# The last eight expert rows in groups of one, and half an addition on GpSimd, in a hybrid-layer and expert kernel

## The reference, cut to what matters

```python
h = _modulate(x, norm_ffn_g, sh2, sc2)          # 256 tokens x 1024
# per token and per head (8 heads): the 16 best of 128 x 128 experts, by sums of two key scores
# idx: 8 x 16 expert numbers a token; gate: softmax over the 16 scores
act = gelu(h . U[idx]) * gate                   # one dot product of 1024 for each chosen expert
x   = x + g2 * sum(act * V[idx])                # weighted sum of the chosen experts' value rows
```

## Time and profile before

| what | value |
|---|---|
| median of 3 runs | 1267.8 us (1267.05 to 1268.56) |
| the profiled execution, its own time | 1268.92 us |
| its span, first to last instruction | 1267.0 us |
| PE busy | 1140.1 us, 90% |
| DVE busy | 865.2 us, 68% |
| ACT busy | 311.8 us, 25% |
| POOL busy | 331.8 us, 26% |
| mean granted TensorE clock | 0.990 |
| the expert rows in the span | from about 603 us to the end |

### The profile page before, as it was taken

One profiled execution on the slowest core, in us unless ns is written; L12 is line 12 of the kernel. 1 busy time (PEld: TensorE's weight loads), 2 busy tenths in 40 slices (PEclk: granted clock), 3 DMA queues, 4 the chain that ended last, 5 costly groups with the idle time before them and its releaser, 6 DMA issues.

```text
span 1267.0 us, 14106 instructions
## 1 busy us (share of the span) xinstructions
PE 1140.1 (90%) x4824; PEld 696.8 (55%) x4824; DVE 865.2 (68%) x2320; ACT 311.8 (25%) x1005; POOL 331.8 (26%) x285
## 2 busy tenths in 40 slices
PE   9999999989999999999999899999777777777777
PEld 6866658767856678786656454554232323323322
DVE  2758735566445787863897777777778777777665
ACT  0125300244111232421232222232222222222222
POOL 0000000000011000000444544545644544454430
PEclk9999999999999999999999999999999999999999
DMA  8851256833145566454999999999999999999995
GB/s 337 312 202 67 100 199 253 309 112 133 67 199 196 208 216 227 191 194 173 373 377 423 423 424 423 423 423 424 424 423 424 423 423 424 423 423 423 423 424 215
DMA packets 54022, 389.10 MB, mean 307 GB/s; under 512 B 8088, under 2 KB 9624, under 8 KB 14784
## 3 DMA queue, kind: packets, MB, share of 16 engines
q0 software_dynamic: 37792, 269.63, 51.4%
q1 hardware_dynamic: 16160, 118.59, 24.6%
HBM read 387.12 MB, written 1.07 MB: 306 GB/s over the span
## 4 chain that ended last, share of the span: by engine, by line
PE 52%; DMA 34%; DVE 10%; ACT 2%; issue 1%; POOL 0%; SPq 0%; DVEq 0%; ACTq 0%
PE bank L566 15%; PE bank L560 13%; DMA wring<-peer_uv_in,arena 11%; DMA arena<-peer_uv_in,arena 9%; PE bank L1153 9%; DMA const<-peer_uv_in,arena 8%; DMA hT<-peer_uv_in,arena 5%; PE bank L1048 2%; PE bank L595 2%; PE bank L968 2%; DVE arena L1644 1%; PE bank L641 1%; DVE arena L1652 1%; PE bank L627 1%; PE bank L791 1%
## 5 line engine op out<-in xcount | busy, mean ns | idle before, releaser
L1153 PE MATMUL bank<-arena 128*128 128x512 f32 x424 | 202.6, 609 | 40.9 <-ACT arena L1609 40.8
L1153 PE MATMUL bank<-wring,arena 128*128 128x512 f32 x376 | 179.1, 610 | 38.8 <-ACT arena L1609 38.8
L566 PE MATMUL bank<-hT,wring 128*128 128x256 f32 (+1 forms) x896 | 172.5, 351 | 1.0 <-ACT arena L1393 1.0
L2442 POOL TENSOR_TENSOR small<-small,const 128x1 f32<-128x1 f32 (+3 forms) x18 | 16.7, 927 | 566.8 <-DVEq L1656 260.1
L2371 DVE CUSTOM_DVE_ANT_0 arena<-arena 128x1024 f32<-128x1024 f32 x106 | 129.3, 1223 | 50.8 <-DMA arena<-peer_uv_in,arena 50.6
L566 PEld LDWEIGHTS bank<-hT,wring 128*128 128x128 f32 x896 | 150.2, 190 | 24.3 <-issue 8.4
L1153 PEld LDWEIGHTS bank<-arena 128*128 128x128 f32 x424 | 78.2, 194 | 150.4 <-issue 80.8
L2481 POOL DMA_INDIRECT arena<-peer_uv_in,arena x104 | 124.8, 1200 | 132.9 <-PE bank L1153 110.8
L2371 DVE CUSTOM_DVE_ANT_0 wring<-wring,arena 128x1024 f32<-128x1024 f32 x94 | 114.7, 1221 | 44.0 <-DMA wring<-peer_uv_in,arena 43.8
L2481 POOL DMA_INDIRECT wring<-peer_uv_in,arena x94 | 113.9, 1211 | 110.1 <-PE bank L1153 98.8
L1153 PEld LDWEIGHTS bank<-wring,arena 128*128 128x128 f32 x376 | 68.3, 191 | 134.7 <-issue 69.9
(11 more groups left out here) (250 smaller groups left out, 1526.7 us busy)
## 6 DMA issues: line engine op xcount, KB each, us to landing
wring<-w_in SPq DMA_DIRECT2D x22, 2048.0 KB, 8.2
wring<-ada_in SPq DMA_DIRECT2D x12, 2048.0 KB, 9.2
wring<-wo_in SPq DMA_DIRECT2D x5, 2048.0 KB, 7.9
wring<-br_in SPq DMA_DIRECT2D x2, 2048.0 KB, 9.3
arena<-pq_in SPq DMA_DIRECT2D x2, 2048.0 KB, 9.8
wring<-w1b_in SPq DMA_DIRECT2D x2, 1120.0 KB, 8.8
const<-const_in SPq DMA_DIRECT2D x1, 2188.5 KB, 17.8
arena<-cmp_in SPq DMA_DIRECT2D x2, 1024.0 KB, 10.9
```

Source lines behind the costliest of these rows:

```text
L566: ins = pe.matmul(bank[:, at:at + n_tok], w[:, k, col:col + P], rhs[:, k, :], start=(k == 0), stop=(k == KC - 1))
L1153: ins = pe.matmul(sums_of[half][:, :], diag[:, at % NDIAG, :], v_row[slot_of[at]][:, half * 512:(half + 1) * 512], start=(n == 0), stop=(n ...
```

## The change

The first hunk gives the product of tile 1, half 0, a tile of its own, `last_scaled`. The second makes rows 248 to 255 eight groups of one (before only 254 and 255 were). The third and fourth take the addition of tile 1, half 0, off DVE: DVE makes the product and goes on, SP waits for a new semaphore `added` for that half, and the count of `result` for the last half becomes 3. The last lets POOL, behind all its gathers, wait for that product and make the addition.

```diff
         scaled = take(512)
+        last_scaled = take(512)
...
-        sizes = [2] * (ROWS // 2 - 1) + [1, 1]
+        SINGLES = 8
+        sizes = [2] * ((ROWS - SINGLES) // 2) + [1] * SINGLES
...
-                    sp.wait_ge(sem("result"), 2 * t + half + 1)
+                    if (t, half) == (1, 0):
+                        sp.wait_ge(sem("added"), 1)
+                    else:
+                        sp.wait_ge(sem("result"), 3 if t else half + 1)
                     sp.dma_start(out[t * P:(t + 1) * P, c], x3[:, t, c]).then_inc(sem("stored"), 16)
...
-                    free(tt(scaled, bank[:, :], gate_ffn[:, c], ALU.mult), ("pv", t, half))
+                    into = last_scaled if (t, half) == (1, 0) else scaled
+                    free(tt(into, bank[:, :], gate_ffn[:, c], ALU.mult), ("pv", t, half))
+                    if (t, half) == (1, 0):
+                        continue
                     taken(dve, ("pv", t, half))
                     link(tt(x3[:, t, c], x3[:, t, c], scaled, ALU.add), "result")
...
+            taken(pool, ("pv", 1, 0))
+            pool.tensor_tensor(x3[:, 1, 0:512], x3[:, 1, 0:512], last_scaled, ALU.add).then_inc(sem("added"), 1)
```

## The result

The changed kernel takes 1274.56 us, the median of 6 runs (1273.01 to 1275.5), against 1267.94 us for the kernel before in the same comparison (1267.05 to 1269.13). The ratio is 1.005, with a 95% interval of 1.0037 to 1.0062. That is a loss of 4.7 to 7.9 us, outside the range given above. The profiled execution took 1274.37 us, 1272.3 of it the span: 5.3 us more than the span of 1267.0 before.

The account below looks back on a forecast made before the run. Gathers were taken to bound the loop, leaving only the tail open, where values, then PE, start the last four rows. Part 1 at 0.0 and part 2 at -0.38 us, from the median 1267.8, gave 1267.4 us; range 1266.4 to 1268.6.

Parts of the forecast that it names:

- part 2: In the tail, moving the first half's last addition from VectorE to GpSimd was forecast to win 0.38 us.
- X - 1.31: Move of the kernel's end in us, X being GpSimd's addition time; a loss from X = 1.31 us on.
- the sum: Whole kernel: 0.0 from the groups of one and -0.38 us from GpSimd's addition, giving 1267.4 us from the median.
- Part 1, gain 0.0: Rows 248 to 253 in groups of one gain 0.0 us, since row 252 still waits for its gathered values.
- The values are the gate: PE's start on row 252 waits for its gathered values, landing at about 1255.2; the rival denying it had 0.06.
- X = 0.93 us: GpSimd's 512-column addition in the tail: 0.39 us of GpSimd's fixed part plus 0.54 of VectorE's columns.
- VectorE waits for GpSimd's end: VectorE's last addition starts only after GpSimd's ends, at 1263.44 us; the rival without this lock had 0.15.
- The stores: SP's last two stores, now 0.7 us apart instead of 1.45: zero cost, up to 0.3 us kept for the range.
- The rival on the other side: GpSimd's addition in the last 2 us is long; slower by over 0.2% above X = 3.8 us (0.04), below that 0.28.
- Slower by over 0.2%, 0.05: Chance of 0.05 that the whole kernel becomes over 0.2% slower, about 2.5 us.

Follow-up runs that it names:

- e1: The kernel before with only rows 248 to 255 put in groups of one, both last additions on VectorE; 1269.37 us against 1269.43, ratio 1.0002.
- e5: The changed kernel with an explicit GpSimd drain between its last gather and its wait for VectorE's product; 1270.49 us, ratio 1.0005 against the kernel before.
- e4: The kernel before with row 255's left half multiplied ahead of row 254's right half on PE; 1268.65 us, ratio 0.9996.

## Why the prediction was wrong

**The step that failed** stands in part 2, "In general the end moves by X - 1.31", and with it fails the sum. It took the end to be VectorE's last addition and its store, and it put GpSimd's coming late to the block's end at nothing, without a reason. The runs show 5.05 us there (7.98 to 13.03 from the last landing), and 3.88 with the wait alone. The wait and the addition were put into GpSimd's queue without asking what is queued behind them there: the block's DRAIN, whose row was in the trace all along, 39.05 us from 1224.0, ending at 1263.0. That row called for the bound that I did not draw: as long as nothing says what a DRAIN does, moving its start from 1230, where the last gather was issued, to 1264 costs between nothing and all of what it does after the last landing, 4.06 us or more. In hindsight the sum, from the last landing, is: VectorE's product ends at 3.36 us, GpSimd starts 0.09 later, adds for 1.26, drains for 8.10, and the engines meet in 0.23: 13.04, measured 13.03. The store's path ended near 7.8 and no longer counted.

Point by point:
- *Part 1, gain 0.0*: right, and for its reason. After the change PE stood idle for 1.70 us ahead of row 252 (1.8 forecast), released by the DMA; row 255's diagonal copy ended at 1259.97, which is 1259.64 on the clock of the kernel before (its gathers landed 0.33 us sooner), against 1259.57 forecast; PE had no gap behind row 252. e1's time (1.0002) allows some 1 us either way; its tail, 7.98 us as before, is what shows the 0.0.
- *The values are the gate*: right. PE's row began 0.14 us behind the landing in e1 and after the change, with the diagonal long ready in both.
- *X = 0.93 us*: too low. It measured 1.26 us in three traces (1.261, 1.259, 1.257). The mix of GpSimd's fixed part with VectorE's columns mis-sized the columns: if the fixed part is 0.39, which no run shows for an addition, they took 0.87 and not 0.54. GPSIMD Engine Reference of the Trainium skill, Elementwise, gives 4497 ns for 2048 columns; the estimate from it is 1.1 us by proportion and 1.4 with 0.39 fixed (the prediction has "some 1.3" and does not say with what). It was the better one: 1.26 us lies between its two ends.
- *VectorE waits for GpSimd's end*: right in kind, mis-sized. VectorE's addition took 1.00 us after the change and 1.71 in e5, where it began 0.1 us after GpSimd's; in both it ended 0.55 us after GpSimd's did (1264.57 - 1264.02, 1265.70 - 1265.16), not 0.73, so of its 0.69 us alone some 0.14 seem to pass beside the other. SBUF — State Buffer of the Trainium skill, Who interferes with whom, has it that a VectorE instruction with two SBUF inputs contends with a GpSimd instruction that reads SBUF, and that such contention is an exclusive lock. The two traces agree but for these 0.14 us. With X = 1.26 the formula gave -0.05; VectorE's end moved by -0.29, of which 0.18 is this and 0.05 the quicker hand-over. That this comes near the -0.38 forecast is partly luck: X was too low by 0.33, and these two terms took 0.23 of it back.
- *The stores*: put at zero, with 0.3 us kept for the range. The second took 2.14 us to land and not 2.01, so of VectorE's 0.29 us only 0.15 reached its landing (7.42 us behind the last gather's, 7.57 before).
- *The rival on the other side*, a long GpSimd addition, had the right engine and the right sign and the wrong instruction. Its threshold, an addition of 3.8 us, was not passed (1.26 us); what held GpSimd for 9.4 us was the DRAIN, which the rival does not name.
- *Slower by over 0.2%, 0.05*: too small a chance for a queue of which I had read only the busy part.

## What to carry to other kernels

Ask of every instruction that is put late into a queue what stands behind it there, and count the block's end as one of its users: the DRAIN is in the instructions of the block's line and in no busy table. An engine that is done early is not free; GpSimd with 260 gathers behind it needed 8 us to close, hidden only because nobody asked it for anything later. Here the tail of 2 us was shortened more cheaply on the engine that makes its input (0.52 us in e4's trace, by the order of two matmuls) than by a further engine.

## What the runs showed of the hardware that was not expected

- GpSimd's DRAIN took 8.07 us after 260 gathers in two kernels in which GpSimd only waited, and 8.10 from the end of its addition in two in which it added, whether it could begin 3.4 us before the last landing or 4.7 us after it. Begun right behind the last gather, it ended 4.04 to 4.06 us after the last landing, in the kernel before and in five of the experiments.
- It grows with the gathers since the last drain, but not in proportion: 0.06 us with no DMA, 0.35 after three DMAs, 1.68 after 20 gathers, 2.91 after 132, and 0.07 right behind another drain. Begun right behind a gather, it ended 2.63 us after the last landing with 128 gathers behind it and 3.24 with 240.
- A 128x512 fp32 addition on GpSimd took 1.26 us, 1.8 times VectorE's 0.69. A VectorE addition begun beside it ended 0.55 us after GpSimd's, in three traces.
